# A hybrid decoder layer in float32 on one core: where the early loads are issued, one block for merge, projection and MLP, and a common residue for operand addresses

## The reference

```
u = rms_norm(h, norm_mix_pre)
proj = u @ w_in                      # q,k,v | z | xbc | dt | mem_q | gate logits
y_sb  = stick_breaking_attention(q, k, v)                  # 16 heads of 64
y_ssd = ssd_branch(z, xbc, dt, ...)  # conv, silu, chunked scan of 32 heads, grouped rms_norm
y_mem = mem_cross_attention(mem_q, mem, norm_mem, w_mem_kv)  # 4 heads of 256, 256 keys
g = sigmoid(gate_logits)             # three gates of 1024
merged = g0 * (y_sb @ w_sb_out) + g1 * (y_ssd @ w_ssd_out) + g2 * (y_mem @ w_mem_out)
h = h + rms_norm(merged @ w_o, norm_mix_post)
ff = square(relu(rms_norm(h, norm_mlp_pre) @ w_up)) @ w_down
h = h + rms_norm(ff, norm_mlp_post)
```

## Time and profile before

| what | value |
|---|---|
| median of 3 runs | 2851.55 us (2851.38 to 2852.48) |
| the profiled execution's own time | 2849.78 us |
| its span, first to last instruction | 2847.7 us |
| mean granted TensorE clock | 0.984 of full |
| TensorE busy | 2724.5 us (96%) |
| front, first matmul to last | 9.4 to 376 us |
| stick-breaking | 376 to 1155 us |
| SSD | 1169 to 1576 us |
| merge | 1598 to 2026 us |
| projection | 2037 to 2132 us |
| MLP, with the last normalization | 2132 to 2848 us |

### The profile page before, as it was taken

The page is one execution under the profiler, slowest core; times in us unless marked ns, Lnnn a source line. Parts: engine busy times, 40 slices in busy tenths (PEclk is TensorE's granted clock), DMA queues, the critical chain, the costliest instruction groups (busy, mean ns, idle before and its releaser), DMA issues. The chain is left out here.

```text
span 2847.7 us, 34568 instructions
## 1 busy us (share of the span) xinstructions
PE 2724.5 (96%) x13268; PEld 2268.6 (80%) x13268; DVE 1497.3 (53%) x1523; ACT 971.9 (34%) x1679; POOL 1441.6 (51%) x777
## 2 busy tenths in 40 slices
PE   6999899999999999799999699999899999999998
PEld 5888678888888888688888577788687888888886
DVE  5100036766677666588888566633264434334343
ACT  4101034444444444566666345432241100101002
POOL 2466534445444544388888524455115535535443
PEclk9999999999999999899999899999999999999999
DMA  3444514242424341467676544343332111111113
GB/s 133 147 167 150 156 69 117 89 141 89 126 89 126 104 126 45 141 199 206 197 206 185 212 143 157 137 141 118 104 111 89 52 38 60 45 45 60 38 48 115
DMA packets 169121, 335.96 MB, mean 118 GB/s; under 512 B 15488, under 2 KB 96000, under 8 KB 168960
## 3 DMA queue, kind: packets, MB, share of 16 engines
q1 hardware_dynamic: 168960, 333.76, 36.3%
HBM read 244.97 MB, written 88.74 MB: 117 GB/s over the span
## 5 line engine op out<-in xcount | busy, mean ns | idle before, releaser
L973 POOL TENSOR_TENSOR sb_beta<-sb_beta,sb_rest 128x128 f32<-128x128 f32 (+7 forms) x128 | 164.2, 1283 | 398.9 <-DVE sb_rest L1033 398.9
L804 PE MATMUL sb_psg<-uh,sb_wl 128*128 128x512 f32 x768 | 312.6, 407 | 0.0
L804 PE MATMUL sb_psg<-ul,sb_wh 128*128 128x512 f32 x768 | 306.5, 399 | 0.0
L804 PE MATMUL sb_psg<-uh,sb_wh 128*128 128x512 f32 x768 | 306.5, 399 | 0.0
L2220 POOL TENSOR_TENSOR ff_mh<-ff_w,one 128x1024 fp32r<-128x1024 f32 x32 | 73.4, 2295 | 399.7 <-PE ff_ps L2273 306.0
L1033 DVE TENSOR_TENSOR_SCAN sb_rest<-sb_rest 128x128 f32<-128x128 f32 (+7 forms) x128 | 183.0, 1430 | 159.3 <-ACT sb_rest L922 158.5
L1769 PE MATMUL mg_ps<-mg_yh,mg_wh 128*128 128x512 f32 x512 | 206.4, 403 | 27.9 <-DVE mg_yl L1974 27.1
L2391 ACT ACTIVATE ff_sq<-ff_ps 128x1024 f32<-128x1024 f32 x32 | 32.9, 1028 | 519.2 <-PE ff_ps L2273 519.2
L2497 DVE TENSOR_TENSOR ff_total<-ff_ps,ff_total 128x1024 f32<-128x1024 f32 x112 | 137.0, 1223 | 133.1 <-PE ff_ps L2309 132.3
L1769 PE MATMUL mg_ps<-mg_yh,mg_wl 128*128 128x512 f32 x512 | 201.6, 394 | 0.0
L1769 PE MATMUL mg_ps<-mg_yl,mg_wh 128*128 128x512 f32 x512 | 201.2, 393 | 0.0
(11 more groups left out here) (279 smaller groups left out, 7211.6 us busy)
## 6 DMA issues: line engine op xcount, KB each, us to landing
sb_w<-in_w_in SPq DMA_DIRECT2D x48, 512.0 KB, 4.8
scratch_proj<-sb_out SPq DMA_DIRECT2D x48, 512.0 KB, 3.0
sb_k<-scratch_qk SPq DMA_DIRECT2D x64, 256.0 KB, 6.3
ssd_arow<-scratch_decay SPq DMA_DIRECT2D x32, 512.0 KB, 5.4
mg_w<-in_w_branch SPq DMA_DIRECT2D x32, 512.0 KB, 4.4
mg_raw<-scratch_y SPq DMA_DIRECT2D x32, 512.0 KB, 4.9
mg_gate<-scratch_proj SPq DMA_DIRECT2D x32, 512.0 KB, 3.6
ff_w<-in_w_up SPq DMA_DIRECT2D x32, 512.0 KB, 3.4
```

Source lines behind the costliest of these rows:

```text
L804: last = nc.tensor.matmul(ps_g[:, h], l[:, s, k], r[:, k, h * HALF:(h + 1) * HALF], start=(k == 0 and j == 0), stop=(k == KB - 1 and j == 2))
L973: nc.gpsimd.tensor_tensor(beta[:, i % 3, 0:cols], beta[:, i % 3, 0:cols], rest[:, i % 3, 0:cols], ALU.mult).then_inc(weighted, 1)
```

## The change

**Early loads.** SP issues `early_loads` after the item whose load ahead is the last one: n + 3 is 39, so n = 36, `("kv", 15)`. Five loads and five stores of the front that stood behind them now stand ahead of them.

**One block.** `merge_branches` and `mix_and_mlp` no longer open blocks but return programs that one block runs one after the other. Parts of the projection's start are given to the merge's loops by slot: SP loads w_o blocks 0 to 2 at slot 52 (once all y are split, since their buffers lie over those of raw y) and 3 to 5 at slot 58; ScalarE rounds w_o blocks 0 to 2 at slot 55, pieces of token tiles 0 and 1 at slots 57 and 63, block 3 at slot 60; VectorE subtracts one slot later each. Token tiles 0 and 1 of `merged` are rounded in three pieces (blocks 0 to 3, 4 to 6, and 7), each once its blocks are summed. w_o's halves lie in the buffers of `dnh`, `dnl`, `fh` and `fl` now; blocks 4 to 7 lie over `mg_yh` and wait for the last merge matmul. The PSUM slots of mix, transposes and up-products are exchanged, so that the mix begins in banks that the memory attention used.

**Addresses.** Tensors are allocated in another order, with odd sizes last, and the two constants `one` and `eps` become views of a tensor of 32 elements. Operands of the long products then lie at one distance from the start, 3328 modulo 4096. By the same counting, before: `uh`, `ul` 3264; the front's weights 3264; stick-breaking's ring 3328, `wth` and `wtl` 3264 and values 3328; SSD's ring 2816; merge 3264 on both sides; projection `mh`, `ml` 3264 and w_o 3584; up 3264 on both sides, down 3584 on both. Two waits of ScalarE for the front's kv stores move from the first sigmoid of the convolution to its first evacuation (`m` = 0), since `padded` lies over `kvout` now.

The diff without its re-indentation, cut to its core:

```diff
@@ front @@
-    v_tile, kv_tile = sb("v", [P, 2, S]), sb("kvout", [P, 2, M])
+    v_tile = sb("v", [P, 2, S])
...
+    kv_tile = sb("kvout", [P, 2, M])
...
-            if ITEMS[n] == ("in", 18):
+            if n + SLOTS == len(ITEMS) - 1:
                 sp.wait_ge(tables_stored, 16 * (1 + 2 * GROUPS))
                 for s in range(2):
                     sp.wait_ge(qk_stored[s], 32 * N_QK // 2)
                 early_loads(sp)
@@ stick_breaking @@
-    padded = sb("padded", [P, CONV - 1 + S])
-    beta, rest = sb("beta", [P, 3, S]), sb("rest", [P, 3, S + 1])
+    beta = sb("beta", [P, 3, S])
     ring = Ring(nc, ctx, "sb", consts)
...
+    n_conv = MQ0 - X0
+    cw, cb = sb("cw", [P, n_conv, CONV]), sb("cb", [P, n_conv])
+    rest, padded = sb("rest", [P, 3, S + 1]), sb("padded", [P, CONV - 1 + S])
...
-                if m == 1:
+                if m < 2:
+                    stored_before, blocks = ((before.kv_stored, KV_BLOCKS), (before.v_stored, V_BLOCKS))[m]
                     for x in range(2):
-                        act.wait_ge(before.v_stored[x], 16 * V_BLOCKS // 2)
+                        act.wait_ge(stored_before[x], 16 * blocks // 2)
@@ ssd @@
+        ring = Ring(nc, ctx, "sg", consts)
+        out_tile = sb("out", [P, 2, S])
+        w = sb("w", [P, 2, R, P])
+        wh, wl = (sb(n, [P, 2, R, P], F32R) for n in ("wh", "wl"))
         a_row, e_pair = sb("arow", [P, 2, R, P]), sb("epair", [P, 4, GB, P])
...
-        ring = Ring(nc, ctx, "sg", consts)
-        out_tile = sb("out", [P, 2, S])
@@ mix_and_mlp @@
-        UP_PS, DOWN_PS = (2, 0), (1, 3)
+    UP_PS, DOWN_PS = (0, 2), (1, 3)
+    FIRST, SECOND, THIRD = slice(0, 4), slice(4, 7), slice(7, 8)
+    M_PIECES = [(t, ks) for ks in (FIRST, SECOND, THIRD) for t in range(2)] + [(t, slice(0, KB)) for t in range(2, TB)]
...
+    wh = [dnh[:, k] for k in range(KEPT)] + [fh[:, k] for k in range(KEPT)]
+    wl = [dnl[:, k] for k in range(KEPT)] + [fl[:, k] for k in range(KEPT)]
+    tile, gain, u, turned_scaled = total[:, 0:3], total[:, 3], total[:, 4:6], total[:, 6]
...
-        mix, turned = acc[:, 0:3], acc[:, 3]
+    mix, turned = [acc[:, 2], acc[:, 3], acc[:, 0]], acc[:, 1]
...
+    def early_loads(sp, slot):
+        if slot == 52:
+            sp.wait_ge(merge.y_split, N_Y)
+            for k in range(3):
+                load_w(sp, k)
+        if slot == 58:
+            for k in range(3, 6):
+                load_w(sp, k)
...
-            for k in range(KB):
-                load_w(k)
+        for k in range(6, KB):
+            load_w(sp, k)
+        sp.wait_ge(merge.w_used, N_Y)
+        sp.wait_ge(merge.summed, N_Y - MERGED_LAST)
...
             for k in range(KB):
                 pe.wait_ge(o_split, k + 1)
                 for t in range(2):
-                    if k == 0:
-                        pe.wait_ge(m_split, t + 1)
+                if k in (FIRST.start, SECOND.start, THIRD.start):
+                    pe.wait_ge(m_split, M_AT[t, k] + 1)
...
+    def round_m(act, n):
+        t, ks = M_PIECES[n]
+        act.wait_ge(merge.summed, N_Y - 2 * KB + ks.stop)
...
+    def early_rounds(act, slot):
+        if slot == 55:
+            for k in range(3):
+                round_w(act, k)
+        if slot == 57:
+            for n in range(0, 2):
+                round_m(act, n)
+        if slot == 60:
+            round_w(act, 3)
+        if slot == 63:
+            for n in range(2, 4):
+                round_m(act, n)
@@ layer @@
-        consts |= {n: sb(ctx, n, [P, 1]) for n in ("one", "eps")}
+        small = sb(ctx, "small", [P, 32])
+        consts |= {"one": small[:, 0:1], "eps": small[:, 1:2]}
...
+            @block.sync
+            def _(sp):
+                merging.sync(sp, early)
+                mixing.sync(sp)
```

More of the change, by code:

```diff
@@ L62 @@
     vector: Any
+@dataclass
+class MergeSignals:
+    y_split: Any
+    w_used: Any
+    summed: Any
+@dataclass
+class EarlyMix:
+    loads: Any
+    rounds: Any
+    rests: Any
 @dataclass
@@ L1544, in _, with merge_branches @@
                                                 ALU.subtract).then_inc(st_split, 1)
-def merge_branches(nc, w_out, proj, kv, y, squares, ssd_gain, merged, consts):
+def merge_branches(nc, ctx, w_out, proj, kv, y, squares, ssd_gain, merged, consts):
     gates_of = (0, 1, 1, 2)
@@ new lines, in score @@
+        def score(u, j):
+            c = u * STEPS + j
+            pe.wait_ge(q_split, u + 1)
+            pe.wait_ge(k_split, u // 2 + 1)
+            if c:
+                pe.wait_ge(e_done, c)
+            for d in range(DB):
+                for x, (l, r) in enumerate(split3((qh, kh), (ql, kl))):
+                    last = nc.tensor.matmul(ps_s[:, 0:M], l[:, d, j * P:(j + 1) * P], r[:, d],
+                                            start=(d == 0 and x == 0), stop=(d == DB - 1 and x == 2))
+            last.then_inc(scores, 1)
@@ new lines, in weigh_values @@
+        def weigh_values(u, d):
+            pe.wait_ge(pt_split, STEPS * (u + 1))
+            pe.wait_ge(v_split, u // 2 + 1)
+            if 2 * u + d:
+                pe.wait_ge(y_out, 2 * u + d)
+            for m in range(MB):
+                for x, (l, r) in enumerate(split3((vh, pth), (vl, ptl))):
+                    last = nc.tensor.matmul(ps_y[:], l[:, m, d * P:(d + 1) * P], r[:, m],
+                                            start=(m == 0 and x == 0), stop=(m == MB - 1 and x == 2))
+            last.then_inc(y_mm, 1)
@@ new lines, in sum_squares @@
+        def sum_squares(g, half):
+            pe.wait_ge(ssq_loaded, 16 * (g + 1))
+            if 2 * g + half:
+                pe.wait_ge(g_rooted, 2 * g + half)
+            nc.tensor.matmul(ps_n[:], consts["ones"][:], ssq[:, half * HALF:(half + 1) * HALF],
+                             start=True, stop=True).then_inc(g_summed, 1)
+        for slot in range(SLOTS):
+            u, j = memory_step(slot)
+            if u is not None:
+                if u and j < 2:
+                    weigh_values(u - 1, j)
+                if u < UNITS:
+                    if j:
+                        turn(u, j - 1)
+                    if j < STEPS:
+                        score(u, j)
+                    if j == 3 and u % 2 == 0:
+                        turn_values(u // 2)
+            for g in range(GROUPS):
+                if slot in (STAT_AT[g], STAT_AT[g] + 1):
+                    sum_squares(g, slot - STAT_AT[g])
+            p, i = divmod(slot, PART)
+            if i < 4:
+                two_blocks(p * KB, i)
+            else:
+                n, h = slot // 2, slot % 2
+                if h == 0:
+                    begin(n)
+                last = passes(n, range(KB), (h,))
+                if h:
+                    last.then_inc(w_used, 1)
```

1666 lines of the change are left out of this document (814 added, 852 removed).

## The result

The changed kernel takes **2815.09 us** (median of 4 runs, 2813.62 to 2818.56), beside 2852.02 us for the kernel before on the same chip: ratio 0.9871, 95% interval 0.9854 to 0.9889, 37 us faster. The forecast was 2800 us in a range of 2794 to 2813, so the sign was right, the gain 14 us too large, and the time 2 us above the range. The profiled execution took 2814.62 us, 35.2 less than that of before.

The account below looks back on a forecast made before the run. TensorE, busy 2724.5 of 2847.7 us, was taken as the bound. Front 14.5, seam 12.8 and placement 23.7 sum to 51.0 us off the 2851.55 us median, rounded to 2800 us; range 2794 to 2813.

Parts of the forecast that it names:

- Front, 14.5 us: Front: moving the 17 early transfers behind the last block removes a 13.04 us TensorE wait and 1.5 of slow clock.
- Seam, 12.8 us: Merge to projection: early w_o loads and splits, without the barrier, save 10.7 us of waiting and 2.1 of slow clock.
- Distance as the cause: Stick-breaking, SSD, projection: operand distance modulo 4096 sets the pace of 512-column matmuls; making it 0 gains 23.7 us.
- the port rule: Rival, all long products: independent operand ports make placement worth 0, leaving 27.3 us of gain, 2824 us; chance 0.10.
- 0.2267 as the new pace everywhere: Long products start 0.2267 us apart after the change; in stick-breaking 2304 starts gain 6.3 ns each, 14.5 us.
- Values: Stick-breaking: 192 value matmuls of 512 columns gain 6.3 ns each, 1.2 us.
- The seam that carried the price: Front to stick-breaking: starts 0.2267 us apart before it, 0.2330 behind, only the weights' buffer changing; source of 6.3 ns.
- SSD, 7.1 us: SSD: 1152 matmuls of 512 columns gain 6.2 ns each once the weight ring's distance is 0.
- the cover: SSD: VectorE splits w 8.7 us before its product starts, against 0.2 us by which each chunk shortens.
- VectorE becomes SSD's pace: SSD: a sign that would show the prediction wrong, VectorE instead of TensorE setting the pace; no size given.
- half of it: Long products: case within the placement rival, another part of the address counts too, half the placement gain; 2812 us.
- late transfers: Rival, stick-breaking's start: early transfers land too late behind stores, costing up to 14.5 us, 2815 us; chance 0.05.

Follow-up runs that it names:

- early: Kernel before with one line changed: stick-breaking's 17 early transfers issued behind the front's last weight block; ratio 0.9942 to the kernel before.
- pad64: Changed kernel with 64 bytes of padding ahead of stick-breaking's ring, so ring and values lie 64 beyond their moving operands again; ratio 0.9901 to the kernel before.
- sq4: Changed kernel with four buffers in place of two for SSD's summed squares; 2809.9 us, ratio 0.9849 to the kernel before.
- ssdold: Changed kernel with SSD's tensors allocated in the order of before, its ring 448 bytes short of uh and ul again; ratio 0.9875 to the kernel before.

## Why the prediction was right and wrong

- **Front, 14.5 us: right.** 15.2 in the profile. The move alone (early) shortened the front by 14.2 in its profile and the kernel by 17 (13 to 20). The last early transfer is issued at 338.52 and, at 16.2 us to its landing, there by 354.7 (forecast 353), 6 us ahead of stick-breaking's first matmul.
- **Seam, 12.8 us: right.** 10.8 up to the first matmul and about 2.1 of clock behind it; the merge's own length did not move (428.6 and 428.5 us), so the gates had the slack that the earlier trace rows gave them.
- **Distance as the cause: right**, against the port rule of the Trainium skill, "TensorE: Matmul & The Clock Gate", section "Step-by-step: what each phase is for". One stage at two distances (pad64) and 16 series by themselves show it. "Modulo 4096" was too much: 256 decides.
- **"0.2267 as the new pace everywhere": this step failed for stick-breaking.** 2304 x 6.3 ns was to give 14.5 us. The products gave 8.3 us (552.6 to 544.3 us of TensorE's time from each of their starts to the next, idle time left out), and of that 1.6 is clock: the profile of before has a stretch at 1.2 GHz in stick-breaking (382.2 to 385.6), that of after none. That leaves 6.7, or 2.9 ns a start. Values gave 0.4 of their 1.2 us; scores, not in the sum, 0.8. The seam that carried the price is one uninterrupted series, while stick-breaking's products stand in 254 series of 5 to 13. The sum needed the pace behind an interruption; before, every start was slow anyway, so nothing in its stick-breaking showed it, but the merge's starts behind its memory attention did: 234, 230, 236, 229, 232, 231 and then 227 ns from 1675.82 on in the timeline of before, where the sum took 226.6 from a stretch late in it. The first six distances here take 1.39 us, the next six 1.36:

```profile
1675.82 0.40 PE L1769 MATMUL mg_ps<-mg_yh,mg_wh 128*128 128x512 f32 x1
...
1677.21 0.39 PE L1769 MATMUL mg_ps<-mg_yh,mg_wh 128*128 128x512 f32 x1
...
1678.57 0.39 PE L1769 MATMUL mg_ps<-mg_yh,mg_wh 128*128 128x512 f32 x1
```

- **SSD, 7.1 us: the term was right, the cover was not.** The gate products shrank by 7.4 us in sq4 (276.2 to 268.8) and 5.5 in the changed kernel. But TensorE's idle time grew from 3.2 to 10.5 us, and the stage's other matmuls took 1.6 more, a stretch of low clock among it. The step that failed is the cover taken from "VectorE has w split by 1218.02 for a product that starts at 1226.70". That was the slack of one input; the bound was another path in the same stage, ScalarE's evacuation behind the state, for which TensorE already waited 1.6 us before and waits 8.0 now. Four buffers or the moved store take it back to 1.4 to 2.3. Some 2.4 to 3.4 us of the new idle time aren't explained by the pace (early, ssdold). "VectorE becomes SSD's pace" stood among the things that would prove me wrong, but no price was put on it as a rival.
- The sum: 51.0 forecast, less 6.4 (stick-breaking) and 10.6 (SSD), plus 1.6 (clock in the MLP's first block) and 0.8 (front), less 1.0 in the gaps, gives 35.4 of the 35.2 us seen. The 2812 named for "half of it" and the 2815 named for late transfers come near what was measured, but by luck: what they were named for did not happen.

## What to carry to other kernels

A price per instruction taken from an undisturbed series holds for series as long; read it also behind the interruptions that the stage has, before multiplying. When the pacing engine gets faster by a fraction of a microsecond a round, look for loops through the other engines and a queue, not only for the slack of its direct inputs: find a wait that repeats each round (before, GpSimd's for the store of the squares: 26.5 us in 18 times) and ask what it holds up. The cheapest cure was then one line: a transfer that is ready early goes ahead of those for which the queue waits.

## What the runs showed of the hardware

- Matmuls of 512 float32r columns with their own weight loads start 226.7, 229.5 or 233.3 ns apart at a distance of 0, 192 or 64 bytes between the two operands in a partition. 256, 448 and 320 bytes gave the same three; moving both operands alike changed nothing.
- At distance 0 the full pace sets in some starts behind narrower matmuls (mostly 3 behind 128 columns, and 5 behind 256, each time 233, 236, 228, 233, 231 and then 226), and at once behind one of the same width. At 512 bytes it took 9.
- A store of 64 KB landed 7.0 us after its issue when 1.3 MB stood ahead of it on SP's queue, and in this kernel that closed a loop through SP, GpSimd, VectorE, ScalarE and TensorE.
